# Keep phase-1 tensors and the FFN1 weights in one SBUF arena, and start three of the eight FFN1 weight groups inside phase 1

## The chip, the cores and the metric

The program runs on all 8 cores of one Trainium2 chip, with no exchange between them. Each core takes four prompt sequences of 256 tokens (1024 rows) and half of a sample's 1024 latent tokens (512 rows of its own, and the other 512 only as keys and values). All cores read the same weights from the chip's memory. The metric is device time in microseconds of the slowest core; lower is better.

## The reference, cut to what matters

One trunk layer: modulation vectors from `silu(cond) @ w_mod + b_mod` (six vectors: three for the attention half, three for the feed-forward half), then two residual sub-layers.

```
def _layer(x, mod, p, ctx_ckv=None, ctx_kr=None, rope=None):
    shift_a, scale_a, gate_a, shift_f, scale_f, gate_f = mod
    h = _rms(x, p['g_attn_pre']) * (1.0 + scale_a) + shift_a
    proj = h @ p['w_in']                      # -> q_lora | kv_lora | k_rope | sgu_u | sgu_v
    ...
    attn = _attend(q, k, val)                 # 8 heads, 64+32 dims
    sgu = _sgu(u, v, p['w_sgu'], p['b_sgu'], p['g_sgu'], p['beta_sgu'])
    mix = jnp.concatenate([attn, sgu], axis=-1) @ p['w_o']
    x = x + gate_a * _rms(mix, p['g_attn_post'])
    h = _rms(x, p['g_ffn_pre']) * (1.0 + scale_f) + shift_f
    f = jnp.square(jax.nn.relu(h @ p['w_ff1'])) @ p['w_ff2']
    x = x + gate_f * _rms(f, p['g_ffn_post'])
    return x, ckv, kr
```

`w_mod` is 1024 x 6144, `w_ff1` 1024 x 4096 and `w_ff2` 4096 x 1024, all f32 in memory. The kernel holds them as bf16.

## The kernel before, in words

The kernel is written as one program with a small recording helper (`KB`). Every operation names the tiles it reads and writes by strings; the helper puts a semaphore wait in front of it for the last writer (and readers) of each name. The order on each engine is the order of the Python code; nothing reorders it.

Three stages follow each other:

- **Stage A (L264 to L443)**: modulation for the attention half. Six slabs of `w_mod` (1024 x 512 each) come through two buffers `wm0`, `wm1`, beside `w_in`, `w_uq`, `w_ukv`, `w_sgu`, `w_o`, and the rotary tables `CT`, `ST` are computed in scratch tiles (`rowi`, `coli`, `ang`, `tmpa`, `m_`, `ti`).
- **Stage B (L445 to L760)**: the attention half. `front_A` loads and normalises 512 rows, `front_B` projects them (`w_in_bf`, `w_uq_bf`) and leaves keys, values and queries, `build_V` makes values, `attention` runs the heads, `sgu_and_out` the gating part and the output projection (`w_o_bf`). It runs once for the sample tokens and then for `g = 0` and `g = 1`, two groups of 512 prompt rows; in each of these, `attention` is called twice (`j = 0, 1`, 256 rows each). In that short-sequence form of `attention`, POOL first copies the rotary rows of all eight heads into the key tiles (`cp("pool", ...)`, L642), and DVE and ACT then cast the other 64 rows into the same tiles (L649, L651). Each cast writes the names `KT.h` that the copies wrote, so it waits for them.
- **Stage C (L762 to L815)**: a barrier of all engines, the close of the SBUF tiles of stages A and B, and the modulation for the feed-forward half: six more `w_mod` slabs, through the one buffer `wm2`. POOL issues all DMAs that convert f32 to bf16, in this order: slab 6, `w1.0`, `w2.0`, slab 7, `w1.1`, `w2.1`, ..., slab 11, `w1.5`, `w2.5`, `w1.6`, `w2.6`, `w1.7`, `w2.7`. Here `w1.g` is 512 columns of `w_ff1` and `w2.g` 512 rows of `w_ff2`, each 1 MiB as bf16, as is a slab. A slab's DMA waits until TensorE has read the slab before it, since the buffer is the same; TensorE's 16 matmuls of a slab (8 chunks for each of two conditions) wait until it has landed. SP issues the two broadcasts of `g_ffn_post` (`G_f`, 128 x 1024 f32 each) and one of `b_mod` a slab (`bm2`, 128 x 512 f32).
- **Stage D (L818 to the end)**: the feed-forward half, six groups of 256 rows. `ff1` and `ff2` are interleaved; chunk `fc` of 32 needs weight group `fc // 4` of both. The program ends with this stage's `tail`.

The loop that sets the order of stage C:

```
    mod2_dma(6)
    wgroup_dma(0)
    for j in range(6, 12):
        emit_mod2(j)
        if j + 1 < 12:
            mod2_dma(j + 1)
        wgroup_dma(j - 5)
    wgroup_dma(7)
    kb.barrier(exclude=("w1.", "w2."))
```

Of the kernel before, what the change touches and what calls it, by code (L numbers as in the profile page):

```python
# [14 lines left out]
D = 1024  # L15
# [124 lines left out]
def build_program(debug=False):  # L140
# [30 lines left out]
    w_ff1 = din("w_ff1", [D, 4 * D])  # L171
# [7 lines left out]
    kb = KB(nc)  # L179
# [26 lines left out]
    def mm(out, lhsT, rhs, start, stop):  # L206
        return lambda e: e.matmul(out, lhsT, rhs, start=start, stop=stop)  # L207
# [11 lines left out]
    def psf(i):  # L219
        return psb[i][:, :]  # L220
# [22 lines left out]
    kb.op("pool", lambda e: e.memset(eps_col[:], EPS), writes=["eps"])  # L243

    P1 = contextlib.ExitStack()
    w_in_bf = kb.sb(P1, "w_in_bf", [128, 8, 1440], BF16)
    wkr_pad = kb.sb(P1, "wkr_pad", [128, 8, 96], BF16)
    wkr_swp = kb.sb(P1, "wkr_swp", [128, 8, 96], BF16)
    w_uq_bf = kb.sb(P1, "w_uq_bf", [128, 2, 8, 96], BF16)
    w_uq_swp = kb.sb(P1, "w_uq_swp", [128, 2, 8, 96], BF16)  # L250
    w_ukv_bf = kb.sb(P1, "w_ukv_bf", [128, 8, 128], BF16)
    wsguT = kb.sb(P1, "wsguT", [128, 8, 128], BF16)
    w_o_bf = kb.sb(P1, "w_o_bf", [128, 8, D], BF16)
    G_a = kb.sb(P1, "G_a", [128, 2, D], F32)
# [3 lines left out]
    bT_bc = kb.sb(P1, "bT_bc", [128, 8, 128], F32)  # L258
    bTb = kb.sb(P1, "bTb", [128, 8, 128], BF16)
    cst_bf = kb.sb(P1, "cst_bf", [128, 128], BF16)  # L260
    CT = kb.sb(P1, "CT", [128, 1024], F32)
    ST = kb.sb(P1, "ST", [128, 1024], F32)

    kb.op("pool", lambda e: e.memset(cst_bf[:], 1.0 / 128.0), writes=["cst_bf"])  # L264

# [9 lines left out]
    kf = kb.sb(T0, "kf", [128, 1], F32)  # L275
    freq = kb.sb(T0, "freq", [128, 1], F32)
    isrow = kb.sb(T0, "isrow", [128, 1], F32)
    rowi = kb.sb(T0, "rowi", [128, 16, 64], F32)
    coli = kb.sb(T0, "coli", [128, 16, 64], F32)
    ang = kb.sb(T0, "ang", [128, 1024], F32)  # L280
    tmpa = kb.sb(T0, "tmpa", [128, 1024], F32)
    m_ = kb.sb(T0, "m_", [128, 1024], F32)
    ti = kb.sb(T0, "ti", [128, 1024], I32)
    wm = [kb.sb(T0, "wm%d" % i, [128, 8, 512], BF16) for i in range(2)]
    bm = [kb.sb(T0, "bm%d" % i, [128, 512], F32) for i in range(2)]
    mrow = [kb.sb(T0, "mrow%d" % i, [128, 512], F32) for i in range(2)]
# [157 lines left out]

    W1 = contextlib.ExitStack()  # L445
    hT = kb.sb(W1, "hT", [128, 8, 512], BF16)
    xq = kb.sb(W1, "xq", [128, 4096], BF16)
    uT = kb.sb(W1, "uT", [128, 4, 512], BF16)
    gv = kb.sb(W1, "gv", [128, 4, 512], F32)
    vn = kb.sb(W1, "vn", [128, 4, 512], BF16)  # L450
# [2 lines left out]
    ckvn_bf = kb.sb(W1, "ckvn_bf", [128, 4, 128], BF16)  # L453
    kr_f = kb.sb(W1, "kr_f", [128, 4, 32], F32)
    cqnT = kb.sb(W1, "cqnT", [128, 2, 512], BF16)
    ckvT = kb.sb(W1, "ckvT", [128, 1280], BF16)
    krT = kb.sb(W1, "krT", [128, 1280], BF16)
    KTh = [kb.sb(W1, "KTh%d" % i, [128, 1280], BF16) for i in range(2)]
    Vt = kb.sb(W1, "Vt", [128, 10, 512], BF16)
    PT = [kb.sb(W1, "PT%d" % i, [128, 512], BF16) for i in range(3)]  # L460
    rec = kb.sb(W1, "rec", [128, 512], F32)
    junk = kb.sb(W1, "junk", [128, 1024], BF16)
# [289 lines left out]
    for g in range(2):  # L752
        slots = [4 + 4 * g + t for t in range(4)]
        front_B(slots, 0, True, 0, None, g * 512)
        build_V([0, 1, 2, 3], lambda kt: kt * 128)
        for j in range(2):
            attention(j * 256, 256, j * 256, 256, 2 * j, j * 256)
        if g == 0:
            front_A(xp[512:1024, :], [8, 9, 10, 11])
        sgu_and_out(slots, 0, None)  # L760

    kb.barrier()  # L762
    W1.close()
    P1.close()

    P2 = contextlib.ExitStack()
    G_f = kb.sb(P2, "G_f", [128, 2, D], F32)
    w1_bf = kb.sb(P2, "w1_bf", [128, 8, 4 * D], BF16)
    w2_bf = kb.sb(P2, "w2_bf", [128, 32, D], BF16)
    for c in range(2):  # L770
        kb.dma("sp", G_f[:, c, :], g_ffn_post.partition_broadcast(128), "G_f%d" % c, True)
# [9 lines left out]
        kb.dma("sp", bm2[:], b_mod[j * 512:(j + 1) * 512].partition_broadcast(128), "bm2", True)  # L781

    def wgroup_dma(g):
        kb.dma("pool", w1_bf[:, :, g * 512:(g + 1) * 512], w_ff1[:, g * 512:(g + 1) * 512].rearrange("(kc p) n -> p kc n", p=128), "w1.%d" % g, True)
        kb.dma("pool", w2_bf[:, g * 4:(g + 1) * 4, :], w_ff2[g * 512:(g + 1) * 512, :].rearrange("(kc p) n -> p kc n", p=128), "w2.%d" % g, True)

    def emit_mod2(j):
# [64 lines left out]
    def ff1(sg, fc):  # L852
        hb_ = h2T[sg % 2]
        b = 2 + fc % 2
        r = fc % 2
        r4 = (sg * NFC + fc) % NH
        kb.group("pe", [mm(psf(b)[:, 0:256], w1_bf[:, kc, fc * 128:(fc + 1) * 128], hb_[:, kc, :], kc == 0, kc == 7) for kc in range(8)],
                 reads=["h2T%d.%d" % (sg % 2, kc) for kc in range(8)] + ["w1.%d" % (fc // 4)], writes=["ps%d" % b])
        act(rl[r][:, :], psf(b)[:, 0:256], AF.Relu, ["ps%d" % b], ["rl%d" % r])
        tt("dve", hid[r4][:, :], rl[r][:, :], rl[r][:, :], ALU.mult, ["rl%d" % r], ["hid%d" % r4])  # L860
# [119 lines left out]
```

How the kernel before makes its waits and increments, by code:

```python
    def _wait(self, engname, ev):  # L50
        if ev is None:
            return
        sem, val = ev
        w = self.waited[engname]
        if w.get(id(sem), 0) >= val:
            return
        w[id(sem)] = val
        self.eng[engname].wait_ge(sem, val)
        self.nwaits += 1
# [26 lines left out]
    def op(self, engname, fn, reads=(), writes=()):  # L86
        self._deps(engname, reads, writes)
        ins = fn(self.eng[engname])
        self.ecount[engname] += 1
        ev = (self.esem[engname], self.ecount[engname])
        ins.then_inc(ev[0], 1)
        self._record(ev, reads, writes)
        self.nops += 1
        return ev
# [1 line left out]
    def group(self, engname, fns, reads=(), writes=()):  # L96
        self._deps(engname, reads, writes)
        ins = None
        for fn in fns:
            ins = fn(self.eng[engname])
            self.nops += 1
        self.ecount[engname] += 1
        ev = (self.esem[engname], self.ecount[engname])
        ins.then_inc(ev[0], 1)
        self._record(ev, reads, writes)
        return ev
# [1 line left out]
    def dma(self, q, out, in_, res, write, **kw):  # L108
        reads = [] if write else [res]
        writes = [res] if write else []
        self._deps(q, reads, writes)
        if res not in self.dsem:
            self.dsem[res] = [self.stack.enter_context(self.nc.semaphore("d_" + res.replace(".", "_"))), 0]
        d = self.dsem[res]
        self.eng[q].dma_start(out=out, in_=in_, **kw).then_inc(d[0], 16)
        d[1] += 16
        ev = (d[0], d[1])
        self._record(ev, reads, writes)
```

## Time and profile before

| what | us |
|---|---|
| two runs of the kernel | 1116.92 and 1202.06, median 1159.49 |
| the profiled execution | 1120.75 |
| its span, slowest core (core 3) | 1119.7 |
| spans of the 8 cores | 1090.8 to 1119.7 |
| PE busy | 744.6 (67%) |
| DVE busy | 435.2 (39%) |
| ACT busy | 345.3 (31%) |
| POOL busy | 81.6 (7%) |

Times in the rows are counted from the span's start on the core that the row belongs to. "PE" is TensorE's matmul part. The page cuts the span in 40 slices of 28 us each; a digit is a busy share in tenths, so the row of DMA shows in which slices transfers run at all, and the row of GB/s what they moved. The chain of waits goes back from the last instruction to whatever released each step, and so names what the end of the program hangs on at each time.

### The profile page before, as it was taken

Reading aid. Unit: us, or ns where it says so; the run is one execution under the profiler, and the core shown is the slowest. Engines: PE = TensorE matmul, PEld = TensorE weight load, DVE = VectorE, ACT = ScalarE, POOL = GpSimd, SP = SyncE. Lnnn points to the kernel's source line nnn. Section 1 sums busy time; section 2 is a strip of 40 time slices with the busy share of each in tenths; the row PEclk is TensorE's granted clock in tenths of the full one; section 3 lists DMA queues with packets and bytes.
Section 4 is the critical chain, followed back from the end, with each engine's and each line's share of the span. In section 5 each row is a group of like instructions: output and inputs, shape, how many; then the busy total and the mean of one; then the engine's idle time right before and its main releaser. Section 6 shows DMA issues by size and latency. Waiting matters only on the chain.

```text
span 1119.7 us, 14484 instructions; the slowest of 8 cores (1090.8 to 1119.7 us)
## 1 busy us (share of the span) xinstructions
PE 744.6 (67%) x4097; PEld 409.8 (37%) x4097; DVE 435.2 (39%) x775; ACT 345.3 (31%) x815; POOL 81.6 (7%) x131
## 2 busy tenths in 40 slices
PE   2224158577767766667671242249999999999995
PEld 1001044122233333332340010027666665656663
DVE  2447231645654157531762123013242424242423
ACT  0000244444534454335421000024243433324322
POOL 3002000011101100010102001200000000000000
PEclk9566568779988865869576556559999999999998
DMA  8997700000000200000003999994000100000000
GB/s 140 167 141 110 230 14 1 0 1 1 1 1 1 88 1 1 1 13 1 1 1 60 162 156 144 151 164 84 2 39 1 39 1 39 2 38 2 31 8 39
DMA packets 38608, 58.05 MB, mean 52 GB/s; under 512 B 4322, under 2 KB 26244, under 8 KB 38532
## 3 DMA queue, kind: packets, MB, share of 16 engines
q0 software_dynamic: 29104, 35.41, 22.1%
q1 hardware_dynamic: 9428, 21.72, 6.9%
q8 instruction: 37, 0.61, 0.2%
q14 instruction: 39, 0.32, 0.1%
HBM read 85.58 MB, written 6.95 MB: 83 GB/s over the span
## 4 chain that ended last, share of the span: by engine, by line
PE 53%; DMA 17%; DVE 11%; ACT 9%; issue 7%; POOL 0%; ACTq 0%; DVEq 0%; SPq 0%; POOLq 0%
PE psb L207 51%; DMA wm<-w_mod 16%; ACT junk L190 3%; ACT PT L190 2%; DVE rec L626 2%; PE psb L210 2%; DVE hT L193 2%; DMA x<-xs 1%; ACT stat L190 1%; DVE xq L197 1%; DVE vn L193 1%; ACT L190 1%; DVE h2T L193 1%; DVE KTh L204 1%; ACT hT L190 1%
## 5 line engine op out<-in xcount | busy, mean ns | idle before, releaser
L207 PE MATMUL psb<-w_bf,hid 128*128 128x512 bf16 x768 | 198.8, 382 | 11.2 <-DVE xn L193 6.3
L207 PE MATMUL psb<-h2T,w_bf 128*128 128x256 bf16 x1536 | 201.8, 276 | 0.9 <-ACT h2T L190 0.9
L207 PE MATMUL psb<-wm,srep 128*128 128x512 bf16 x192 | 70.5, 549 | 171.1 <-DMA wm<-w_mod 164.6
L207 PEld LDWEIGHTS psb<-h2T,w_bf 128*128 128x128 bf16 x1536 | 151.8, 99 | 60.6 <-issue 2.2
L193 DVE TENSOR_TENSOR hid<-rl 128x256 bf16<-128x256 f32 x192 | 80.7, 425 | 222.1 <-PE psb L207 135.1
L190 ACT ACTIVATE rl<-psb 128x256 f32<-128x256 f32 x192 | 73.1, 384 | 223.0 <-PE psb L207 175.2
L207 PEld LDWEIGHTS psb<-wm,srep 128*128 128x128 bf16 x192 | 24.5, 132 | 216.6 <-issue 212.5
L207 PEld LDWEIGHTS psb<-w_bf,hid 128*128 128x128 bf16 x768 | 73.2, 98 | 64.1 <-issue 15.9
L190 ACT ACTIVATE PT<-psb 128x512 bf16<-128x512 f32 x112 | 65.4, 596 | 57.7 <-PE psb L207 54.7
L207 PE MATMUL psb<-PT,Vt 128*128 128x512 bf16 (+1 forms) x144 | 57.3, 398 | 28.2 <-ACT PT L190 13.7
L193 DVE TENSOR_TENSOR mrow<-psb,bm 128x512 f32<-128x512 f32 x24 | 16.6, 691 | 144.4 <-PE psb L207 143.4
L626 DVE RECIPROCAL rec<-psb 64x256 f32<-64x256 f32 (+1 forms) x24 | 54.8, 2284 | 18.8 <-PE psb L207 18.4
L190 ACT ACTIVATE junk<-psb 128x512 bf16<-128x512 f32 (+2 forms) x76 | 37.5, 494 | 69.6 <-PE psb L207 66.7
L207 PE MATMUL psb<-PT,ones_bf 128*128 128x512 bf16 (+1 forms) x144 | 58.3, 405 | 0.0
L190 ACT ACTIVATE xn<-x 128x1024 bf16<-128x1024 f32 x12 | 12.6, 1053 | 147.0 <-DVE G_f L193 146.4
L207 PE MATMUL psb<-w_in_bf,hT 128*128 128x416 bf16 (+2 forms) x224 | 49.5, 392 | 3.2 <-DVE hT L198 3.2
L207 PE MATMUL psb<-xq,KTh 96*128 96x512 bf16 (+1 forms) x144 | 50.0, 408 | 0.0
L207 PE MATMUL psb<-w_o_bf,hT 128*128 128x512 bf16 x192 | 43.7, 387 | 6.7 <-DVE hT L193 5.6
L190 ACT ACT_TABLE_LOAD x10 | 12.8, 1283 | 105.1 <-DVE tmpa L193 49.3
L207 PEld LDWEIGHTS psb<-PT,Vt 128*128 128x128 bf16 x144 | 16.4, 114 | 72.1 <-issue 68.0
L204 POOL COPY KTh<-krT 32x256 bf16<-32x256 bf16 (+1 forms) x40 | 21.8, 564 | 203.7 <-DVE KTh L204 115.0
L204 DVE CAST KTh<-psb 64x512 bf16<-64x512 f32 (+1 forms) x32 | 19.7, 616 | 39.6 <-PE psb L207 38.0
(158 smaller groups left out, 819.8 us busy)
## 6 DMA issues: line engine op xcount, KB each, us to landing
w_bf<-w_ff POOLq DMA_DIRECT2D x16, 1024.0 KB, 28.9
wm<-w_mod POOLq DMA_DIRECT2D x12, 1024.0 KB, 16.1
x<-xs SPq DMA_DIRECT2D x8, 512.0 KB, 13.1
x<-xp SPq DMA_DIRECT2D x8, 512.0 KB, 5.0
yp<-x SPq DMA_DIRECT2D x8, 512.0 KB, 2.6
bm<-b_mod SPq DMA_DIRECT2D x12, 256.0 KB, 9.0
w_in_bf<-w_in POOLq DMA_DIRECT2D x1, 2880.0 KB, 51.5
w_o_bf<-w_o POOLq DMA_DIRECT2D x1, 2048.0 KB, 26.2
```

The source lines that it names most:

```text
L190: return kb.op("act", lambda e: e.activation(out=out, in_=in_, func=func, **kw), reads, writes)
L193: return kb.op(eng, lambda e: e.tensor_tensor(out=out, in0=in0, in1=in1, op=op), reads, writes)
L197: return kb.op(eng, lambda e: e.tensor_scalar(out=out, in0=in0, scalar1=s1, scalar2=None, op0=op0), reads, writes)
L204: return kb.op(eng, lambda e: e.tensor_copy(out, in_), reads, writes)
L207: return lambda e: e.matmul(out, lhsT, rhs, start=start, stop=stop)
L210: return lambda e: e.transpose(out, in_, ident)
L626: kb.op("dve", lambda e: e.reciprocal(out=rec[po:po + 64, 0:nq], in_=den), reads=["ps%d" % pden], writes=["rec%d" % (h % 2)])
```

## The change

One tile `arena` (128 partitions x 32768 bf16, 64 KiB a partition) is allocated for the whole program in place of `w1_bf`. Its eight eighths hold `w1.0` to `w1.7` in stage C and D. In stages A and B its first part holds `w_in_bf`, `CT`, `ST`, `Vt`, `xq`, `KTh`, `ckvT`, `krT`, `w_uq_bf` and `w_ukv_bf`, in this order, and in stage A the scratch of the rotary tables lies over the part from `Vt` on. The first three groups of `w_ff1` lie over `w_in_bf` and the first part of `CT`.

The new function `w1_early` makes POOL wait for everything that the four compute engines have been given up to that place, and then issues the DMAs of `w1.0`, `w1.1` and `w1.2`. It is called in `g == 1`, behind the last `front_B` (the last reader of `w_in_bf`). Stage C issues only `w1.3` to `w1.7`, the barrier in front of it does not wait for the early ones, and `w1.g` now lies as [8][512] in its eighth instead of in columns of one wide tile.

```
@@ -223,6 +223,14 @@
     x1 = kb.sb(PS, "x1", [128, 12, D], F32)
+    arena = kb.sb(PS, "arena", [128, 32768], BF16)
+    _aoff = [0]
+
+    def aview(n_bf16):
+        o = _aoff[0]
+        _aoff[0] = o + n_bf16
+        assert _aoff[0] <= 32768
+        return arena[:, o:o + n_bf16]
@@ -243,12 +251,19 @@
-    w_in_bf = kb.sb(P1, "w_in_bf", [128, 8, 1440], BF16)
+    w_in_bf = aview(8 * 1440).rearrange("p (k n) -> p k n", k=8)
+    CT = aview(2048).bitcast(F32)
+    ST = aview(2048).bitcast(F32)
+    Vt = aview(10 * 512).rearrange("p (t n) -> p t n", t=10)
+    xq = aview(4096)
+    KTh = [aview(1280), aview(1280)]
+    ckvT = aview(1280)
+    krT = aview(1280)
+    w_uq_bf = aview(2 * 8 * 96).rearrange("p (c h d) -> p c h d", c=2, h=8)
+    w_ukv_bf = aview(8 * 128).rearrange("p (h d) -> p h d", h=8)
...
@@ -464,6 +473,15 @@
+    w1v = arena[:, :].rearrange("p (g k n) -> p g k n", g=8, k=8)
+
+    def w1_early(groups):
+        for e_ in ("pe", "act", "dve", "pool"):
+            if kb.ecount[e_] > 0:
+                kb._wait("pool", (kb.esem[e_], kb.ecount[e_]))
+        for g_ in groups:
+            kb.dma("pool", w1v[:, g_, :, :], w_ff1[:, g_ * 512:(g_ + 1) * 512].rearrange("(kc p) n -> p kc n", p=128), "w1.%d" % g_, True)
@@ -752,6 +770,8 @@
         front_B(slots, 0, True, 0, None, g * 512)
+        if g == 1:
+            w1_early([0, 1, 2])
         build_V([0, 1, 2, 3], lambda kt: kt * 128)
...
@@ -759,13 +779,12 @@
-    kb.barrier()
+    kb.barrier(exclude=("w1.",))
     W1.close()
     P1.close()
 
     P2 = contextlib.ExitStack()
     G_f = kb.sb(P2, "G_f", [128, 2, D], F32)
-    w1_bf = kb.sb(P2, "w1_bf", [128, 8, 4 * D], BF16)
     w2_bf = kb.sb(P2, "w2_bf", [128, 32, D], BF16)
@@ -781,7 +800,8 @@
     def wgroup_dma(g):
-        kb.dma("pool", w1_bf[:, :, g * 512:(g + 1) * 512], w_ff1[:, g * 512:(g + 1) * 512].rearrange("(kc p) n -> p kc n", p=128), "w1.%d" % g, True)
+        if g >= 3:
+            kb.dma("pool", w1v[:, g, :, :], w_ff1[:, g * 512:(g + 1) * 512].rearrange("(kc p) n -> p kc n", p=128), "w1.%d" % g, True)
         kb.dma("pool", w2_bf[:, g * 4:(g + 1) * 4, :], w_ff2[g * 512:(g + 1) * 512, :].rearrange("(kc p) n -> p kc n", p=128), "w2.%d" % g, True)
```

**POOL, stage B, `g == 1`, before and with the change.** The rows stand between the last cast of `ckvn_bf` in `front_B` and the residual add of `sgu_and_out`; `KTh<-krT` (now `arena<-arena`) are the copies of the rotary rows, eight for `j = 0` and eight for `j = 1`. Before:

```order
L204 CAST ckvn_bf<-ckvn_f 128x128 [waits s_dve,s_pool] x4
L204 COPY KTh<-krT 32x256 [waits s_dve,s_pe]
L204 COPY KTh<-krT 32x256 [waits s_pe]
L204 COPY KTh<-krT 32x256 [waits s_act,s_pe]
L204 COPY KTh<-krT 32x256 [waits s_pe] x3
L204 COPY KTh<-krT 32x256 [waits s_act,s_pe]
L204 COPY KTh<-krT 32x256 [waits s_pe]
```

With the change:

```order
L204 CAST ckvn_bf<-ckvn_f 128x128 [waits s_dve,s_pool] x4
L115 DMA arena<-w_ff 128x8x512 [waits s_pe,s_act,s_dve,s_pool]
L115 DMA arena<-w_ff 128x8x512 x2
L204 COPY arena<-arena 32x256 x8
L204 COPY arena<-arena 32x256 [waits s_dve,s_pe]
L204 COPY arena<-arena 32x256 [waits s_pe]
```

Three DMA issues and their wait for all four engines now stand ahead of the eight copies of `j = 0`.

**POOL, stage C.** The difference in the order, from the residual adds at the end of stage B on; `wm` is the slab, `w_bf 128x8x512` (now `arena`) a group of `w_ff1` and `w_bf 128x4x1024` one of `w_ff2`:

```order
 L193 TENSOR_TENSOR x<-x,gv 128x512 x4
 L115 DMA wm<-w_mod 128x8x512
-L115 DMA w_bf<-w_ff 128x8x512
 L115 DMA w_bf<-w_ff 128x4x1024
 L115 DMA wm<-w_mod 128x8x512
-L115 DMA w_bf<-w_ff 128x8x512
 L115 DMA w_bf<-w_ff 128x4x1024
 L115 DMA wm<-w_mod 128x8x512
-L115 DMA w_bf<-w_ff 128x8x512
 L115 DMA w_bf<-w_ff 128x4x1024
```

Behind slabs 6, 7 and 8 stands one weight group instead of two. From slab 9 on the order is the same as before.

## Rows read from the trace of the kernel before

**Rows 1.** The page, 40 slices of the span: granted TensorE clock, DMA share, GB/s.

```profile
PEclk9566568779988865869576556559999999999998
DMA  8997700000000200000003999994000100000000
GB/s 140 167 141 110 230 14 1 0 1 1 1 1 1 88 1 1 1 13 1 1 1 60 162 156 144 151 164 84 2 39 1 39 1 39 2 38 2 31 8 39
```

**Rows 2.** The view of all cores: span and mean granted clock.

```profile
core 0: 1090.8 us, clock 0.813
...
core 3: 1119.7 us, clock 0.802
```

**Rows 3.** Chain of waits, core 3: start, us, engine and tile; a DMA's length is issue to landing.

```profile
601.37 20.18 DMA wm<-w_mod
621.69 5.83 PE psb L207 x16
628.04 16.20 DMA wm<-w_mod
...
651.62 14.28 DMA wm<-w_mod
...
672.51 16.08 DMA wm<-w_mod
...
695.96 15.99 DMA wm<-w_mod
...
719.56 14.06 DMA wm<-w_mod
733.96 6.01 PE psb L207 x16
...
752.15 22.86 PE psb L207 x156
```

**Rows 4.** Stretches, core 3: busy by engine, then granted clock, DMA share, GB/s.

```profile
600.00:622.00 22.00, 0.31 (x1) 0.14 (x2) 0.00 (x0) 0.00 (x0) 2.56 (x3) 0.50 0.80 121
622.00:740.00 118.00, 36.40 (x96) 12.45 (x94) 25.60 (x62) 0.00 (x0) 15.88 (x19) 0.59 1.06 153
...
753.00:760.00 7.00, 7.00 (x49) 5.20 (x48) 2.13 (x5) 2.31 (x6) 0.00 (x0) 0.79 1.17 208
...
800.00:1119.00 319.00, 297.00 (x2046) 197.84 (x2044) 108.58 (x226) 106.40 (x280) 0.00 (x0) 0.98 0.05 21
```

**Rows 5.** DMA issues of 602.2:603.0 and of 628.9:629.7 (w1.0, w1.1), us to landing.

```profile
w_bf<-w_ff POOLq DMA_DIRECT2D x1, 1024.0 KB, 28.2
...
w_bf<-w_ff POOLq DMA_DIRECT2D x1, 1024.0 KB, 23.8
```

**Rows 6.** One stretch of core 0, columns as in Rows 4.

```profile
590.00:600.00 10.00, 2.37 (x6) 0.90 (x7) 0.00 (x0) 0.00 (x0) 0.00 (x0) 0.50 1.21 214
```

**Rows 7.** Chain of waits, core 0.

```profile
585.59 11.91 DMA wm<-w_mod
...
723.87 6.68 PE psb L207 x48
```

**Rows 8.** Timeline of POOL, core 3: start, us for all of the row's instructions.

```profile
503.01 2.79 POOL L204 COPY KTh<-krT 32x256 bf16<-32x256 bf16 x8 [7.02 <-DVE krT L204]
...
602.29 1.64 POOL L115 DMA_DIRECT2D w_bf<-w_ff  x2
...
720.43 4.92 POOL L115 DMA_DIRECT2D w_bf<-w_ff  x6
```

**Rows 9.** Timeline of core 3 where attention of `g = 1`, `j = 0` begins.

```profile
529.32 0.20 ACT L190 ACTIVATE stat<-stat 128x4 f32<-128x4 f32 x1
...
531.13 0.68 DVE L204 CAST KTh<-psb 64x512 bf16<-64x512 f32 x1 [1.63 <-PE psb L207]
...
532.26 0.59 ACT L190 ACTIVATE KTh<-psb 64x512 bf16<-64x512 f32 x1 [0.93 <-PE psb L207]
...
534.28 1.06 ACT L190 ACTIVATE PT<-psb 128x512 bf16<-128x512 f32 x2
```

More of the change, by code:

```diff
@@ L245, in build_program @@
     P1 = contextlib.ExitStack()
-    w_in_bf = kb.sb(P1, "w_in_bf", [128, 8, 1440], BF16)
+    w_in_bf = aview(8 * 1440).rearrange("p (k n) -> p k n", k=8)
[8 more added lines that the diff above has]
+    w_ukv_bf = aview(8 * 128).rearrange("p (h d) -> p h d", h=8)
     wkr_pad = kb.sb(P1, "wkr_pad", [128, 8, 96], BF16)
     wkr_swp = kb.sb(P1, "wkr_swp", [128, 8, 96], BF16)
-    w_uq_bf = kb.sb(P1, "w_uq_bf", [128, 2, 8, 96], BF16)
     w_uq_swp = kb.sb(P1, "w_uq_swp", [128, 2, 8, 96], BF16)
-    w_ukv_bf = kb.sb(P1, "w_ukv_bf", [128, 8, 128], BF16)
     wsguT = kb.sb(P1, "wsguT", [128, 8, 128], BF16)
@@ L260, in build_program @@
     cst_bf = kb.sb(P1, "cst_bf", [128, 128], BF16)
-    CT = kb.sb(P1, "CT", [128, 1024], F32)
-    ST = kb.sb(P1, "ST", [128, 1024], F32)
     kb.op("pool", lambda e: e.memset(cst_bf[:], 1.0 / 128.0), writes=["cst_bf"])
@@ L277, in build_program @@
     isrow = kb.sb(T0, "isrow", [128, 1], F32)
[L278 to L283, printed above, removed]
+    _sb = 15616
+    rowi = arena[:, _sb:_sb + 2048].bitcast(F32).rearrange("p (a b) -> p a b", a=16)
+    coli = arena[:, _sb + 2048:_sb + 4096].bitcast(F32).rearrange("p (a b) -> p a b", a=16)
+    ang = arena[:, _sb + 4096:_sb + 6144].bitcast(F32)
+    tmpa = arena[:, _sb + 6144:_sb + 8192].bitcast(F32)
+    m_ = arena[:, _sb + 8192:_sb + 10240].bitcast(F32)
+    ti = arena[:, _sb + 10240:_sb + 12288].bitcast(I32)
     wm = [kb.sb(T0, "wm%d" % i, [128, 8, 512], BF16) for i in range(2)]
@@ L446, in build_program @@
     hT = kb.sb(W1, "hT", [128, 8, 512], BF16)
-    xq = kb.sb(W1, "xq", [128, 4096], BF16)
     uT = kb.sb(W1, "uT", [128, 4, 512], BF16)
@@ L455, in build_program @@
     cqnT = kb.sb(W1, "cqnT", [128, 2, 512], BF16)
[L456 to L459, printed above, removed]
     PT = [kb.sb(W1, "PT%d" % i, [128, 512], BF16) for i in range(3)]
@@ L856, in ff1 @@
         r4 = (sg * NFC + fc) % NH
-        kb.group("pe", [mm(psf(b)[:, 0:256], w1_bf[:, kc, fc * 128:(fc + 1) * 128], hb_[:, kc, :], kc == 0, kc == 7) for kc in range(8)],
+        kb.group("pe", [mm(psf(b)[:, 0:256], w1v[:, fc // 4, kc, (fc % 4) * 128:(fc % 4 + 1) * 128], hb_[:, kc, :], kc == 0, kc == 7) for kc in range(8)],
                  reads=["h2T%d.%d" % (sg % 2, kc) for kc in range(8)] + ["w1.%d" % (fc // 4)], writes=["ps%d" % b])
```

## The prediction, made before the changed kernel was run

> **What bounds the kernel now.** I read the page's slices first. DMA is busy in three places only: the first 140 us, a single slice near 370 us, and slices 22 to 28, about 600 to 770 us [rows 1]. In the last of these the granted TensorE clock stands at its lower level of 1.2 GHz (digits of 5 and 6), because TensorE mostly waits. Next come the cores: the slowest is core 3 with 1119.7 us, the fastest core 0 with 1090.8 [rows 2]. The sum is made against core 3.
>
> Then the chain of waits in order of time. From 601.37 us it is six times the same link: a `w_mod` slab is issued, lands 20.18, 16.20, 14.28, 16.08, 15.99 and 14.06 us later, and TensorE works some 6 us on it before the next slab can be issued into the same buffer [rows 3]. The reader should see that TensorE's 16 matmuls are the small part, and that a slab of 1 MiB takes twice as long as it should. At the 153 GB/s of that stretch [rows 4] a slab (1.049 MB) and its `bm2` (0.262 MB) need 8.6 us. The rest is what stands in front: `w1.1` was issued at 628.9 us and landed 23.8 us later [rows 5], at 652.7, after slab 8 had been issued at 651.62, and `w2.1` stood behind it. So POOL's queue is served in order, and 5.5 to 7.6 us of weights lie ahead of each slab. DMA share is 1.06 in this stretch: transfers bound stage C. Behind it, stage D runs from 752.15 us [rows 3] to the end at the upper clock level with PE busy for 297 of 319 us [rows 4]; it is TensorE's own and of fixed length.
>
> **What is taken out of stage C.** Three DMAs of 1.049 MB leave the queue, behind slabs 6, 7 and 8. By bytes alone that is 3.15 MB / 153 GB/s = 20.6 us. Step by step, on core 3:
> - Slab 6 lands as before, near 621.6: ahead of or beside it are only `G_f` (2 x 0.524 MB), `bm2` and itself, 2.36 MB, which at 121 GB/s [rows 4] take 19.5 us of the 20.18. Slab 7 goes out at 628.04. Until then 22 x 0.121 + 6 x 0.153 = 3.6 MB have moved, against 4.46 MB issued before and 3.41 MB now, so it finds an empty queue: 8.6 + 0.7 (20.18 less 19.5, the start) = 9.3 us in place of 16.20.
> - From a landing to the next issue it is 6.5 to 7.6 us [rows 3], 7.1 as a mean. So slabs 8 and 9 are issued at 644.4 and 660.8 (before 651.62 and 672.51). Each period now holds 2.36 MB, 15.4 us at 153 GB/s, within its 16.4 us, so both land in 9.3 us.
> - Behind slab 9 two groups follow again. Slab 10 is issued at 677.2 (before 695.96) with 3.41 - 16.4 x 0.153 = 0.90 MB ahead and needs 14.5 us; slab 11 is issued at 698.8 (before 719.56) with 1.0 MB ahead, needs 15.2, and lands at 714.0 instead of 733.6.
>
> **Gain 19.6 us**, just under the 20.6 by bytes, since the queue is nearly full even in the short periods. First the row: core 3 shares the chip with seven others, and its rate in this stage is 153 GB/s written, twice that read since the source is f32 [rows 4]. The Trainium skill (HBM Reference, Specifications) gives each of two paired cores about 358 GB/s; as an estimate from that page this would be 179 GB/s written, and the removed bytes would be worth 17.6 us and not 20.6. The measured rate decides here.
>
> **What is late next.** Stage D starts about 18 us sooner, near 734 us. The last three pairs of groups (6.3 MB, 41 us) follow slab 11, so the last lands near 755 us. Stage D takes 1119.7 - 752.15 = 367.6 us for 192 chunks, 1.91 us each, so group 5 is asked for 38 us and group 7 54 us after its start, 772 and 788. No new wait. In 753 to 760 us PE was busy for 7.00 of 7.00 us beside 208 GB/s [rows 4], so transfers beside it cost it nothing.
>
> **What is put into stage B.** POOL's wait is over when ACT ends the last `stat` of `front_B`, 529.32 + 0.20 = 529.5 us [rows 9]. A pair of issues takes 1.64 us and six take 4.92 [rows 8], so three end at 532.0. Only then come the eight key copies, 2.79 us together [rows 8], which before had been done at 503 us, long ahead of need. The first two end at 532.8, the fourth at 533.5, the eighth at 534.9. The casts that wait for them began at 531.13 (DVE) and 532.26 (ACT) [rows 9]; now at 532.85 and 533.55. The second of them holds the PSUM bank that the fourth key product needs, and the fourth cast waits for the eighth copy, so the first exponentials slip from 534.28 [rows 9] to about 535.6. **Cost 1.5 us**, bounds 0 and 5 (nearly the whole of issues plus copies, 2.5 + 2.8). It is on the path: from here to the barrier one engine waits for the other. SP issues nothing here.
>
> A row first: beside DVE's casts nothing of POOL's issuing shows in stage B; the issues that are seen take 0.82 us each [rows 8]. The Trainium skill (SBUF — State Buffer, SBUF: two separate sides) holds that POOL cannot write its descriptors while DVE runs an operation in a two-port mode. By that rule each issue might wait out one 0.69 us cast, an estimate of 2 us more, and the sum would be 1105. No row here shows it.
>
> The early transfers themselves take 14.7 us (at core 0's 214 GB/s [rows 6]) to 20.6 us, from 530 to at most 553. The DMA row is empty there until 600 us [rows 1], which is the cover: 47 us. The 1 KiB runs per weight row stay what they were; the other tiles moved into the arena keep their names and so their waits; the rotary scratch in the arena is used as before. They add no instruction, and I cost them at nothing.
>
> **Sum.** 1120.75 - 19.6 + 1.5 = 1102.65, so **1103 us** for an execution like the profiled one (1.6% less). The median shown, 1159.49, lies 3.5% above the profiled execution because one of its two runs took 1202.06; the other took 1116.92. My numbers are for executions like 1116.92 and 1120.75. A measurement of this kernel tells about 2%, 22 us, from no change.
>
> **Rivals.**
> 1. *The transfers get faster too.* Core 0 came first to stage C, at 585.59 us, had 214 GB/s [rows 6] and its first slab in 11.91 us [rows 7], where core 3 needed 20.18. If every core had 190 GB/s all along, slab 6 would land after 12 us, slabs 7 to 9 after 7.6, slabs 10 and 11 after some 10.5, and with 7.1 us between each landing and the next issue slab 11 would land 12 + 3 x 7.6 + 2 x 10.5 + 5 x 7.1 = 91 us after the first issue instead of 132: 1081. 25 MB less over eight cores may bring them half way there, **1092**. Against: the short periods still ask 144 GB/s on each core, so the load hardly falls. 0.17.
> 2. *The slab hardly waits for those bytes.* If slab and later groups are served side by side, or latency and not queue makes the 16 us, each of three periods loses only what lies between the slab's landing and the next issue. For it: `w1.0` landed 28.2 us after issue [rows 5], 9 us behind slab 6, more than its own 6.9. I put the gain at 3 us a period, 9 in all, net 7: **1113**. 0.10.
> 3. *Slower: the clock in stage D.* Stage D runs at 0.98 granted clock [rows 4], after 150 us in which TensorE mostly rested. If a shorter rest made the chip grant less, its 367.6 us would stretch. Below 0.934 the gain is gone (367.6 x 0.98 / 0.934 = 385.7); at 0.90 it is +33, net +15, **1135**; past 0.88 it is more than 2% slower. Against: core 0 spent 138 us from its first slab to stage D (585.59 to 723.87 [rows 7]) and core 3 151 us, and stage D took 366.9 and 367.6 us. 0.04.
> 4. *The early weights aren't early*, because POOL reaches its wait late or the new barrier holds it up: no gain, plus 1.5: **1122**. Against: the order of POOL's rows; POOL is idle there. 0.03.
>
> **Chances and range.** The forecast has 0.66, with a range of its own of 1096 to 1109: gain 13 to 24 in stage C (20.6 us at 153 GB/s; 26 at 121; less if periods grow), cost 0 to 5. The whole range is 1090 to 1118: it takes in the second rival and the near half of the first. Faster by over 2% (below 1098) are the first rival and the best part of the forecast, 0.16 + 0.08 = 0.24; slower by over 2% is the far part of the third, 0.02; the rest, 0.74, is within 2%.
>
> **What would show it.** Between landing of slab 7, 8 and 9 and their issues 9 to 10 us instead of 14 to 16; slabs 10 and 11 nearly as before. DMA busy in slice 19 or 20. The stretch from first slab issue to stage D 131 us instead of 151. On POOL three issues of about 0.8 us near 531 us and then eight copies; the first exponentials 1 to 2 us later against the end of `front_B`. Stage D 367 us. I am wrong if the slabs still take 14 us or more with an empty queue, if the rate rises above 180 GB/s, or if stage D changes length.

## The result: 0.8% faster, in the range but less than forecast

The changed kernel takes 1108.09 us (median of 15 executions), the kernel before 1118.31 us (median of 14). The ratio is **0.9917, 95% interval 0.9893 to 0.9941**. The 1159.49 us shown ahead came from one of its two executions, at 1202.06; such executions, which both kernels have, are left out of every ratio here. The forecast was 1103 us with 1090 to 1118, and "within 2%" as the likeliest outcome.

The page of the changed kernel, with the three rows that answer to [rows 1], shows that the early transfers are where they were put: the 20th slice has become busy, and slices 22 to 26, the first of stage C, move fewer bytes than before (54 to 147 GB/s; [rows 1] have 60 to 162). The transfers still end in the 28th slice on this core.

```profile
PEclk9666578779988865869567566569999999999998
DMA  8997700000000200000802889994000000000000
GB/s 147 163 143 124 229 1 1 0 1 1 1 1 3 86 1 1 1 13 1 114 1 54 106 132 134 147 158 82 1 39 1 39 1 39 2 38 2 36 4 39
```

The view of all cores answers to [rows 2]. The cores have changed places: the slowest is now core 1, and core 3 (1089.8 us) is among the fast ones. Which core is slow is a matter of the execution, so a comparison of one core with itself misleads here.

```profile
core 1: 1114.0 us, clock 0.807
...
core 4: 1088.5 us, clock 0.814
```

I therefore cut each core's span at four places that its trace shows (the last cast of `ckvn_bf` in `front_B`, the issue of slab 6, the first FFN1 matmul, the end) and took the mean over the eight cores. "B end" goes from that cast to the issue of slab 6; it holds all that the early issues could disturb.

```
mean of 8 cores, us    B end   stage C   stage D   mean span
before                 105.8   145.9     367.3     1108.9
changed                109.9   131.6     367.3     1100.0
```

So stage C gives 14.3 us, stage B takes 4.1, stage D is untouched, and 10.2 us should be left. The medians differ by 10.2 us, the ratio stands for 9.3, and the two mean spans differ by 8.9, because the part ahead of the first cut came out 1.4 us longer. Each row is one execution of each kernel, and stage C differs by some 3 us between executions of the same queue order (145.9, 143.1 and 142.7 further down), so the 14.3 us is good to about that, and the exact match with the medians is luck. Forecast for the three were 19.6, 1.5 and 0.

**Stage C.** The chain of waits of core 1, columns as in [rows 3]. Its stage C, 144.0 us, is the longest of the eight; the shortest is 123.3.

```profile
602.94 18.54 DMA wm<-w_mod
621.62 6.24 PE psb L207 x16
628.38 15.10 DMA wm<-w_mod
...
649.76 12.55 DMA wm<-w_mod
...
669.38 12.35 DMA wm<-w_mod
...
687.83 18.30 DMA wm<-w_mod
...
713.60 15.58 DMA wm<-w_mod
```

And two of core 3's rows in the same execution:

```profile
617.72 10.55 DMA wm<-w_mod
...
635.08 10.69 DMA wm<-w_mod
```

The reader should see the second to fourth slab: 15.10, 12.55 and 12.35 us on one core and 10 to 11 on the other, where [rows 3] have 14 to 16. As a mean of the cores, issue to landing went as follows.

```
slab            6      7      8      9      10     11
before          16.0   16.4   15.4   15.4   14.8   15.8
changed         15.4   12.0   10.8   11.2   15.3   16.1
forecast        20.2    9.3    9.3    9.3   14.5   15.2   (for core 3)
```

The stretch 622 to 740 us of core 1, as in [rows 4], now has less than a full DMA share, 0.92 and 132 GB/s against 1.06 and 153. The queue runs dry between slabs, so this is a mean over full and empty times; a rate while the queue is full stands further down:

```profile
622.00:740.00 118.00, 34.03 (x96) 11.81 (x94) 27.14 (x65) 2.79 (x6) 14.10 (x17) 0.63 0.92 132
```

**Stage B.** POOL's timeline of core 1, which answers to [rows 8], has three issues and then the eight copies, which before were done at 505.80 us, 25 us ahead of the first cast that needs them ([rows 8], [rows 9]):

```profile
527.54 2.68 POOL L115 DMA_DIRECT2D arena<-w_ff  x3 [34.20 <-ACT arena L190]
530.26 2.79 POOL L204 COPY arena<-arena 32x256 bf16<-32x256 bf16 x8
```

The rows that answer to [rows 9] show the hand-over: both casts now wait for POOL.

```profile
531.10 0.68 DVE L204 CAST arena<-psb 64x512 bf16<-64x512 f32 x1 [4.24 <-POOL arena L204]
...
531.77 0.59 ACT L190 ACTIVATE arena<-psb 64x512 bf16<-64x512 f32 x1 [3.10 <-POOL arena L204]
...
533.80 1.06 ACT L190 ACTIVATE PT<-psb 128x512 bf16<-128x512 f32 x2
```

From the last table load of `front_B` (524.99 us here, 527.63 before) to these exponentials it is 8.8 us; before it was 6.65 (to 534.28 in [rows 9]). That is 2.2 us. Most of the other 2 stands some 45 us later in the output projection. The chain of core 3 before and of core 1 now, one row each:

```profile
579.23 7.08 PE psb L207 x32
```

```profile
579.12 8.76 PE psb L207 x32
```

Same 32 matmuls, 1.7 us longer. The windows view of these microseconds and of the four ahead of them says why (granted clock in the third column from the end; 1.00 is the upper level, 2.4 GHz, 0.50 the lower, 1.2 GHz). Before:

```profile
575.00:579.00 4.00, 1.81 (x29) 1.49 (x27) 3.62 (x6) 0.00 (x0) 0.00 (x0) 1.00 0.00 0
579.00:583.00 4.00, 3.77 (x18) 1.79 (x19) 0.08 (x1) 0.80 (x3) 0.00 (x0) 1.00 0.01 4
```

Now:

```profile
575.00:579.00 4.00, 1.78 (x25) 1.53 (x22) 3.34 (x5) 0.00 (x0) 0.00 (x0) 0.91 0.00 0
579.00:583.00 4.00, 3.88 (x11) 1.48 (x12) 0.00 (x0) 0.21 (x1) 0.00 (x0) 0.57 0.02 4
```

In both kernels the clock is at the lower level while TensorE works on the gating part, and reaches the upper one 3 to 4 us ahead of the projection. Then TensorE rests for about 2 us. Before, the clock stays up through the projection. Now it falls again as the projection begins and is back some 3.5 us later. It is a second fall, not a first rise that comes late. Where the expectations below say that the clock "comes back later in the output projection", this fall is what they mean.

### The profile page after: what moved, and what is told of

It reads as the page before. It is cut to its first block, busy times and chain, and to the rows that moved or that the text cites. A ratio compares the mean times of both kernels' runs of the same rounds, so it can differ in the third digit from the quotient of the medians.

```text
span 1114.0 us, 14477 instructions; the slowest of 8 cores (1088.5 to 1114.0 us)
## 1 busy us (share of the span) xinstructions
PE 743.6 (67%) x4097; PEld 409.7 (37%) x4097; DVE 435.1 (39%) x775; ACT 345.1 (31%) x815; POOL 81.6 (7%) x131
## 4 chain that ended last, share of the span: by engine, by line
PE 54%; DMA 16%; DVE 12%; ACT 9%; issue 7%; POOL 1%; DVEq 0%; ACTq 0%; POOLq 0%
PE psb L207 52%; DMA wm<-w_mod 14%; ACT junk L190 3%; ACT PT L190 2%; DVE rec L644 2%; PE psb L210 2%; DVE arena L204 1%; DVE hT L193 1%; DMA ck_ld<-ckr 1%; DVE arena L197 1%; ACT stat L190 1%; DVE vn L193 1%; DVE h2T L193 1%; ACT arena L190 1%; ACT L190 1%
## 5 line engine op out<-in xcount | busy, mean ns | idle before, releaser
L207 PE MATMUL psb<-w_bf,hid 128*128 128x512 bf16 x768 | 198.8, 382 | 11.2 <-DVE xn L193 6.3
L207 PE MATMUL psb<-h2T,arena 128*128 128x256 bf16 x1536 | 201.4, 275 | 0.9 <-ACT h2T L190 0.9
L207 PE MATMUL psb<-wm,srep 128*128 128x512 bf16 x192 | 66.4, 522 | 166.6 <-DMA wm<-w_mod 148.8
L207 PEld LDWEIGHTS psb<-h2T,arena 128*128 128x128 bf16 x1536 | 151.6, 99 | 60.4 <-issue 2.2
L207 PE MATMUL psb<-arena 96*128 96x512 bf16 (+3 forms) x218 | 72.9, 412 | 32.3 <-DVE arena L204 25.1
L207 PE MATMUL psb<-PT,arena 128*128 128x512 bf16 (+1 forms) x144 | 57.3, 398 | 28.3 <-ACT PT L190 14.1
L204 DVE CAST arena<-psb 64x512 bf16<-64x512 f32 (+4 forms) x51 | 32.8, 644 | 100.9 <-PE psb L207 57.0
L207 PE MATMUL psb<-arena,hT 128*128 128x416 bf16 (+2 forms) x224 | 49.1, 389 | 3.2 <-DVE hT L198 3.2
L207 PEld LDWEIGHTS psb<-arena 96*128 96x128 bf16 (+1 forms) x218 | 24.4, 117 | 63.5 <-issue 49.1
L207 PEld LDWEIGHTS psb<-PT,arena 128*128 128x128 bf16 x144 | 16.4, 114 | 72.2 <-issue 68.1
## 6 DMA issues: line engine op xcount, KB each, us to landing
wm<-w_mod POOLq DMA_DIRECT2D x12, 1024.0 KB, 15.4
x<-xs SPq DMA_DIRECT2D x8, 512.0 KB, 11.5
```

The lines of the kernel that those rows point to most:

```text
L204: return kb.op(eng, lambda e: e.tensor_copy(out, in_), reads, writes)
```

## The experiments

The theory after the result: stage C gave less than forecast because a slab's own landing costs more than I put down, and stage B cost more because POOL's copies stand behind the issues, which also makes the clock fall in the output projection. Each was set against rivals. One table holds the stage means of one execution each and the ratios; the run with long rows is read by its landings alone. Neither that run nor the one with one bias row computes the layer: each leaves a part out.

```
kernel                          B end  stage C  stage D   ratio to before (95%)
changed                         109.9  131.6    367.3     0.9917 (0.9893 to 0.9941)
nothing early                   106.0  143.1    367.7     0.9997 (0.9973 to 1.0020)
issued behind the copies        105.8  129.2    367.4     0.9849 (0.9822 to 0.9876)
slabs 6 to 9 alone in queue     109.9  127.2    367.4     0.9867 (0.9838 to 0.9897)
four groups early               109.3  124.5    367.3     0.9837 (0.9802 to 0.9873)
slabs first                     109.9   67.9    388.7     0.9532 (0.9503 to 0.9560)
slabs first, nothing early      105.7   67.6    409.0     0.9694 (0.9662 to 0.9726)
all together                    105.7   67.9    379.7     0.9427 (0.9398 to 0.9455)
delay only, nothing early       109.6  142.7    367.4     1.0062 (1.0035 to 1.0088)
slabs alone, one bias row       109.9  116.8    367.8     0.9802 (0.9763 to 0.9841)
```

### Nothing early

```
-            w1_early([0, 1, 2])
+            w1_early([])
...
-        if g >= 3:
+        if g >= 0:
```

> The arena, its addresses and POOL's wait behind the last front_B are kept, but no weight group is issued early; stage C issues all eight groups of w_ff1 as before the change. Theory (only the moved transfers matter): the stretch from the last ckvn_bf cast to the first slab issue is 105.7 us on nearly every core, as before, stage C is about 146 us as a mean of the cores, and the time is within 0.5% of the kernel before. Rival (the tiles' new places in SBUF cost something): the stretch stays near the 109.9 us of the changed kernel, and the time is 0.3% or more above the kernel before.

Measured: B end 106.0, stage C 143.1 (145.9 before; such means differ by some 3 us between executions), ratio 0.9997. The arena, its addresses and POOL's wait cost nothing that can be measured; all of the effect, both signs, comes from the three moved issues and their transfers. The rival falls.

### Issued behind the key copies

The call moves into `attention`, behind the loop of the eight copies.

```
-        if g == 1:
-            w1_early([0, 1, 2])
...
                 cp("pool", kbuf[64:96, kc0:kc0 + nk], krT[64:96, k0:k0 + nk], krblk, ["KT.%d" % h_])
+            if behind_copies is not None:
+                behind_copies()
...
-            attention(j * 256, 256, j * 256, 256, 2 * j, j * 256)
+            attention(j * 256, 256, j * 256, 256, 2 * j, j * 256, (lambda: w1_early([0, 1, 2])) if (g, j) == (1, 0) else None)
```

> The three early issues stand behind the eight key copies of j = 0 instead of ahead of them. Theory (the copies queued behind POOL's issues cost stage B its 4.2 us, 2.2 directly at the start of attention and 2 because the TensorE clock comes back later in the output projection): the stretch from the last ckvn_bf cast to the first slab issue falls from 109.9 to 105.7 to 107 us on all cores, stage C stays near 132 us as a mean, and the time is 3 to 4 us below the changed kernel, 0.988 of the kernel before. Rival (the 2 us in the output projection come from the transfers running beside attention): it falls only to about 107.9. Second rival (all 4.2 us come from the transfers): it stays at 109.9.

Measured: B end 105.5 to 105.7 on seven of eight cores (107.0 on one), ratio 0.9849 against 0.9917, where 0.988 was expected. POOL's timeline of core 3 shows the issues in their new place, and its chain the output projection at its old length:

```profile
526.51 2.68 POOL L115 DMA_DIRECT2D arena<-w_ff  x3 [26.18 <-DVE arena L204]
529.16 0.77 POOL L204 COPY arena<-arena 32x256 bf16<-32x256 bf16 x2
```

```profile
573.76 7.08 PE psb L207 x32
```

The transfers still run beside attention and cost it nothing. Stage C, 129.2 us, has the queue order of the changed kernel, whose 131.6 it differs from by no more than executions do. The core with 107.0 us has the long output projection (8.56 us), with nothing queued ahead of its copies. All 4.1 us were the price of queueing compute behind three DMA issues, and none of it had to be paid. Both rivals fall.

### Delay only

Three clears of dead tiles take the place of the three issues; POOL waits for them, then come the copies.

```
-            w1_early([0, 1, 2])
+            w1_early([])
+            for nm_, t_ in (("w_uq_swp", w_uq_swp), ("wkr_pad", wkr_pad), ("wkr_swp", wkr_swp)):
+                kb.op("pool", lambda e, t_=t_: e.memset(t_[:], 0.0), writes=[nm_])
+            kb._wait("pool", (kb.esem["pool"], kb.ecount["pool"]))
```

> No weight group is issued early, but POOL clears three tiles that nobody reads any more at the same place, ahead of the key copies of j = 0, about 2.7 us as long as the three issues. Theory (the clock in the output projection comes back later because the start of attention is delayed, not because transfers run beside it): the stretch from the last ckvn_bf cast to the first slab issue is 109 to 110 us, as with the change, and stage C about 145 us. Rival (delay and transfers are both needed): 107.5 to 108.

Measured: B end 109.6 on all cores but one (109.7), without a single transfer. From the table load to the first exponentials it is 8.5 us, 1.9 more than before. The ratio, 1.0062 (1.0035 to 1.0088), has the 3.8 us at the lower end of its interval. The chain of core 3 has the long output projection again:

```profile
573.07 8.77 PE psb L207 x32
```

The clock falls there as in the changed kernel:

```profile
573.00:577.00 4.00, 3.93 (x11) 1.48 (x12) 0.00 (x0) 0.58 (x1) 0.00 (x0) 0.57 0.02 4
```

So some 2 us of delay at the start of attention suffices to make the clock fall again in the output projection, 45 us behind it, and that costs some 2 us more. The traces of all runs show how far this reaches. The long projection (8.4 to 8.8 us, against 6.9 to 7.1) stands on all 48 cores of the six runs with three issues or three clears ahead of the copies, and on 4 of 40 where the copies come first or nothing is issued early: one core of the kernel before (its 107.0 us), two with nothing early, one with the issues behind the copies. So the fall occurs without the delay too, but rarely; with it, it is the rule. Why, no run here tells. (The run with four issues stands apart; see there.)

### Slabs alone in the queue

```
     def wgroup_dma(g, late=False):
...
+        if g < 3 and not late:
+            return
         kb.dma("pool", w2_bf[:, g * 4:(g + 1) * 4, :], ...
...
+        if j == 11:
+            for g_ in range(3):
+                wgroup_dma(g_, True)
         wgroup_dma(j - 5)
```

> w2.0, w2.1 and w2.2 are issued behind slab 11 and w1.5, w2.5, so that slabs 6 to 9 have POOL's queue to themselves. Theory (a slab's own bytes are slow, about 115 GB/s with its bias rows, whatever follows it in the queue): slabs 7, 8 and 9 still take 9.5 to 11 us from issue to landing against 10 to 12.5. Rival (the group issued 0.9 us behind a slab is served beside it): they fall to 7.5 us or less. Slab 6 should then fall by more than the others, since G_f goes beside it. The sum of bytes is the same, and stage D may now wait for w2.0, so that the time is about that of the changed kernel, 0.985 to 1.0 of the kernel before.

Measured, issue to landing for slabs 6 to 9 as means of the cores: 12.1, 9.8, 10.2, 11.7 us, against 15.4, 12.0, 10.8, 11.2. One core's chain:

```profile
611.83 9.88 DMA wm<-w_mod
...
629.07 10.37 DMA wm<-w_mod
```

An empty queue ahead and behind still leaves 9.8 to 10.2 us: the group issued behind a slab is not served beside it, or only little. What it takes is 2.2 us of slab 7, 0.6 of slab 8 and 3.3 of slab 6 against the changed kernel, and 1.4, 0.3 and 1.6 against the run with the issues behind the copies, which has the same order in stage C (13.7, 11.2 and 10.5 us); up to half of these amounts is then a matter of the execution. Slab 9 has lost `w2.2` ahead of it here and keeps two groups behind it, as with the change, and is no better off: 11.7 us is above what was expected (9.5 to 11), 9.9 to 10.5 us on four cores and 12.7 to 14.5 on the other four. Stage D, 367.4 us, waited for none of the late groups.

### One bias row

```
-        kb.dma("sp", bm2[:], b_mod[j * 512:(j + 1) * 512].partition_broadcast(128), "bm2", True)
+        if j == 6:
+            kb.dma("sp", bm2[:], b_mod[j * 512:(j + 1) * 512].partition_broadcast(128), "bm2", True)
```

> As the run with slabs 6 to 9 alone in POOL's queue, but only slab 6 loads bias rows; slabs 7 to 11 add slab 6's bias (their part of the computation is left out). It tells what the 0.26 MB broadcast beside each slab costs. Theory (it costs its bytes, 1.7 us at 153 GB/s, or about 2 at the slab's own rate): slabs 7, 8 and 9 land in 8 to 8.5 us instead of 9.5 to 10.5, stage C is 4 to 6 us shorter, about 122 us as a mean. Rival (a slab alone is what takes 9.5 to 10 us; the broadcast goes beside it for nothing): 9.5 us or more. Second rival (the broadcast holds the slab up out of proportion): 7 us or less.

Measured, in two executions: slabs 7 and 8 in 8.2 and 8.3 us. The broadcast costs each of them 1.6 to 1.9 us, its bytes and no more. A slab by itself takes 8.2 us. Stage C is 116.8 us, 10.4 less than with all bias rows, where 4 to 6 were expected: slabs 9, 10 and 11, with groups in the queue, gained 2.2, 1.6 and 2.7 us (slab 9 took 9.5 us, not 8 to 8.5). Why they gained more than the bytes of a broadcast is open.

```profile
610.57 8.28 DMA wm<-w_mod
...
625.25 8.29 DMA wm<-w_mod
```

### Long rows

Each slab's DMA reads 512 whole rows of `w_ff2` instead of pieces of `w_mod`.

```
-        kb.dma("pool", wm2[:], w_mod[:, j * 512:(j + 1) * 512].rearrange("(kc p) n -> p kc n", p=128), "wm2", True)
+        kb.dma("pool", wm2[:, :, :].rearrange("p k n -> p (k n)").rearrange("p (k n) -> p k n", k=4), w_ff2[(j - 6) * 512:(j - 5) * 512, :].rearrange("(kc p) n -> p kc n", p=128), "wm2", True)
```

> As the run with slabs 6 to 9 alone in POOL's queue, but each slab's DMA reads 512 whole rows of w_ff2, 4 KiB each, in place of 1024 pieces of 2 KiB out of w_mod (the second modulation is so left out). Theory (a slab is slow because of its short pieces; w2 groups landed some 5 us apart in a full queue where w1 groups took 8 to 9): slabs 7, 8 and 9 land in 7 to 8 us instead of 9.5 to 10.5. Rival (a megabyte alone takes that long whatever its rows, by start, rate limit and neighbours): 9.5 us or more.

Measured: slabs 7 and 8 in 9.4 and 9.5 us as means, 0.4 to 0.7 less than with short pieces, from one execution. My theory (7 to 8) falls; the rival (9.5 or more) holds but for 0.1 us.

```profile
631.52 9.63 DMA wm<-w_ff
```

### Four groups early

`w_uq_bf` goes beside `CT` and `ST`, the rotary scratch moves up by its size, and:

```
-            w1_early([0, 1, 2])
+            w1_early([0, 1, 2, 3])
...
-        if g >= 3:
+        if g >= 4:
```

> w_uq_bf is placed beside CT and ST in the arena, so that four eighths are dead behind the last front_B, and w1.0 to w1.3 are all issued there. Theory (each group of w_ff1 taken out of stage C saves some 5 us there, and each issue ahead of the key copies costs 0.9 us at the start of attention): stage C falls by 4 to 6 us to about 127 us as a mean, stage B's last stretch grows from 109.9 to 110.8, net 0.3 to 0.5% below the changed kernel, 0.987 of the kernel before. Rival (stage C is no longer bound by what stands in the queue but by each slab's own landing and TensorE's work): stage C falls by less than 2 us and the time doesn't fall.

Measured: stage C 124.5, 7.1 us less than with three groups; slab 10 now lands in 11.5 us instead of 15.3. Against the 129.2 us of the run with three groups behind the copies it is 4.7 us less, so a group taken out of a slab's way is worth about 5 to 7 us, and executions don't tell that from the 4.8 us a group that the first three gave.

B end was expected at 110.8 us and is 109.3 as a mean. The direct delay grew as expected: from the table load to the first exponentials it is 9.7 us, 3.0 more than before. But the clock falls in the output projection on three cores only; the other five keep it up. A core with the short projection and one with the long one:

```profile
576.40 7.08 PE psb L207 x32
```

```profile
577.17 8.66 PE psb L207 x32
```

The five have 108.7 or 108.8 us, the three 110.1 to 110.3. Four issues ahead of the copies thus cost five of eight cores less than three did: a longer delay isn't always a dearer one.

### Slabs first

If slabs are what the chain waits for, the better change is to the order of the queue. All six slabs are issued at once, into places that no weights fill yet; the weight groups follow. The second text below is for the same order with nothing issued before stage C.

```
+    def slab(j):
+        if j == 6:
+            return wm2[:, :, :], "wm2"
+        if j < 11:
+            return w1v[:, j - 3, :, :], "w1.%d" % (j - 3)
+        return w2_bf[:, 28:32, :].rearrange("p a n -> p (a n)").rearrange("p (k n) -> p k n", k=8), "w2.7"
...
+    kb.dma("sp", bm_all, b_mod[6 * 512:12 * 512].partition_broadcast(128), "bm_all", True)
...
+    for j in range(6, 12):
+        mod2_dma(j)
+    for g in range(4):
+        wgroup_dma(g)
+    for j in range(6, 12):
+        emit_mod2(j)
+    for g in range(4, 8):
+        wgroup_dma(g)
```

> As the changed kernel, but all six slabs are issued at once at the start of stage C, into tiles that no weight fills yet (the old slab buffer, the last four eighths of the arena and the place of w2.7), the six bias rows come as one broadcast, and all other weight groups are issued behind them. Theory (stage C's length is the bytes that stand ahead of slab 11 plus six times a round trip of landing, TensorE and issue): 8.9 MB instead of 16.7 MB go ahead of slab 11 and the round trips overlap, so slab 11 lands some 60 to 70 us after the first issue and stage C takes 80 to 88 us; the 13.6 MB behind it end 150 to 160 us after the first issue, group 7 is asked for at 138, and stage D grows from 367 to 375 to 390 us. Stage B stays at 109.9 us. Time 0.97 of the kernel before (0.96 to 0.98). Rival (transfers bound C and D together, so that what C gives D takes): C + D stay near 495 us, the time is 0.99.

> Slabs first, but no weight group is issued before stage C. It tells what the early groups are worth once no slab waits for a weight group: 16.8 MB follow the slabs instead of 13.6, so they end 175 to 185 us after the first issue. Theory (then the early groups are worth their bytes in stage D, 3.15 MB or some 20 us): stage B 105.7 us, stage C 80 to 88, stage D 395 to 410, the time 0.98 to 0.985 of the kernel before. Rival (stage D keeps up with the weights as they land, so that early groups are worth nothing): stage D within 5 us of that of the run with three early groups, time 0.965.

Measured: stage C falls by half, to 67.9 us; stage D grows by 21.4 to 388.7; ratio 0.9532, below the 0.96 to 0.98 expected. The chain of core 3 has one long wait for the last slab in place of six:

```profile
602.41 0.92 POOL wm L115
603.33 3.46 POOL arena L115 x4
606.79 49.45 DMA w_bf<-w_mod
656.59 3.63 PE psb L207 x16
...
672.51 23.55 PE psb L207 x156
```

Slab 11 lands at 656.24, 53.8 us after the first issue: 8.9 MB at 165 GB/s. I had expected 60 to 70 us, at 130 to 150 GB/s. With nothing early, stage C is the same (67.6) and stage D takes 409.0, 20.3 us more for 3.15 MB: the early groups are then worth their bytes at 155 GB/s. Its ratio, 0.9694, is also below what was expected (0.98 to 0.985). The rival of that run (nothing) falls; so does the one of the first (C + D is 456.6, not 495).

This edit changes two things: what stands ahead of the slabs, and that six slabs no longer take turns in one buffer, each waiting for TensorE to read the one before. No run has the order alone. An estimate from the rows: with slab 6 at 12.1 us, five more at the 10 us of an empty queue, and the 50.8 us of stage C in the changed kernel that are not landings, the stage would take 113 us. By that some 19 of the 64 us belong to the order and some 45 to the slabs landing one behind the other without a round trip.

### All together

Slabs first, four early groups, issued behind the key copies.

> Slabs first as in the run beside it, four early groups instead of three, and the early issues behind the key copies of j = 0. If the three gains add (4.2 us in stage B, 1 MB less behind the slabs, the slabs' 25 us): stage B's last stretch 105.7 us, stage C 80 to 88 us, stage D 370 to 382 us, the time 0.958 of the kernel before (0.95 to 0.97). Rival (stage D's granted clock falls because TensorE waits for weights in its first 60 us): stage D over 390 us and no gain over the run beside it.

Measured: B end 105.7, stage C 67.9, stage D 379.7, **1049.68 us, ratio 0.9427 (0.9398 to 0.9455)**, 5.7% below the kernel before. On the page DMA is dense from the 24th to the 28th slice, and the clock's digits reach 8 and 9 within them:

```profile
PEclk9767567959998785586956858799999999999998
DMA  8999810000000020000083199998101001010101
```

The gains add, and to more than I had put down (0.958, with 0.95 to 0.97). Stage D's clock suffers little: 0.94 in the 92 us in which weights still arrive, with PE busy for 81.6 us of them, where the first 92 us of stage D had 0.98 and 89.6 on core 3 before; 0.97 behind it:

```profile
668.00:760.00 92.00, 81.61 (x540) 54.65 (x549) 27.35 (x58) 29.39 (x76) 0.00 (x0) 0.94 0.74 116
760.00:1046.00 286.00, 264.00 (x1803) 177.46 (x1834) 94.51 (x198) 93.93 (x247) 0.00 (x0) 0.97 0.05 20
```

## Why the prediction was right in kind and off in size

**What bounds the kernel: right.** Stage C hangs on slabs that stand behind weights in one queue. Slabs 7 to 9 fell from 15 to 16 us to 11 to 12, and slabs 10 and 11 stayed, as the step had it. Rival 3 (the clock in stage D) is refuted by 367.3 us on both sides and rival 4 (not early) by the 20th slice of the page. Rival 1 (faster transfers) did not come: in full it wanted slab 6 in 12 us and slabs 7 to 9 in 7.6, and they took 15.4 and 11 to 12. Rival 2 (the slab hardly waits for those bytes) put the gain at 3 us a period; slabs 7, 8 and 9 gained 4.4, 4.6 and 4.2. Its total of 9 us is as far from the measured 14.3 as the forecast's 19.6 is. What refutes it as a mechanism is the run with the slabs alone: a group behind slabs 7 and 8 takes 2.2 us of them at most, so most of the old wait was for what stood ahead.

**The gain in stage C: the term that was mis-sized, 19.6 forecast, 14.3 measured.** First, a slab in an empty queue was put at 9.3 us, from the bytes at 153 GB/s. Alone it takes 9.8 to 10.2 (8.2 for itself and 1.6 to 1.9 for its bias rows), and with a group behind it and neighbours at work 10.8 to 12.0: over three slabs 34.0 us instead of 27.9, 6.1 us short. The empty queue's own rate is some 2 of these, the other traffic some 4. Second, slab 10 was to gain 1.5 us and lost 0.5. Against these 8 us stand some 3 that went better: slab 6 fell by 0.6, slab 11 lost 0.3 and not 1.1, and 1.3 us lie outside the landings. That I reckoned on core 3 doesn't explain the miss: its slabs 7 to 9 took 46.6 us before, those of the mean core 47.2. Its stage C was longer (150.8 against 145.9) through slab 6, 20.18 us against 16.0, which the forecast left as it was. So the 131 us on record for stage C, which meets the measured mean of 131.6, is luck.

The Trainium skill's pair share (HBM Reference, Specifications), by which the bytes were worth 17.6 us, goes by a rate of 179 GB/s written. The changed kernel's stage C shows rates on both sides of it while the queue is full. Core 1 has 160 GB/s at 680 to 690 us. Ten microseconds each on core 3, which came to stage C early, and on core 4:

```profile
600.00:610.00 10.00, 0.00 (x0) 0.00 (x0) 0.00 (x0) 0.00 (x0) 0.67 (x1) 0.50 1.07 221
```

```profile
640.00:650.00 10.00, 3.58 (x10) 1.35 (x11) 0.04 (x1) 0.00 (x0) 0.00 (x0) 0.53 1.13 199
```

Over all cores, the stretches of 5 us from 15 us after slab 6's issue on in which the DMA share was 1.05 or more have 171 GB/s as a mean, 166 before. That the skill's 17.6 us came nearer than 20.6 is no support for it: the gain fell short through single landings, not through the rate of a full queue.

**The cost in stage B: 1.5 forecast, 4.1 measured.** The mechanism was right and its place: casts wait for copies behind three issues. One row was misread on the way: the old copies were done at 505.80 us, not at 503, where they began; nothing hangs on it. The direct part was 2.2 us, since POOL started 0.7 us after ACT's last `stat` and each hand-over added a tenth or two. The other 2 us were not in the sum: the clock's second fall, in the output projection. I had written that the cost stays within 0 and 5, and it did. The Trainium skill's rule (SBUF — State Buffer, SBUF: two separate sides), by which DVE's work could hold up descriptor writing, was not put to the test here: on core 1 DVE was idle from 526.86 to 531.10 us, all through the three issues. With the issues behind the copies one cast fell among them:

```profile
527.30 0.68 DVE L204 CAST arena<-psb 64x512 bf16<-64x512 f32 x1 [0.98 <-PE psb L207]
```

They took 2.68 us there too, 0.89 each, against 0.82 in [rows 8]. The estimate of 2 us more doesn't show.

**Late next: right.** Stage D takes 367.3 us as before; no weight was late.

**Sum.** -14.3 + 4.1 = -10.2 us. On record: -18. The measured 1108 lies within the forecast's own 1096 to 1109, near its end: both terms missed to the same side, by 5.3 and 2.6 us.

## What to carry to other kernels

Ask first which transfer the path waits for and what stands ahead of it in its queue. Taking three of sixteen weight groups out of the way was worth 14 us; issuing all awaited slabs ahead of the weights, each into its own place, was worth 64 in that stage and 42 net, with the same bytes. And look at what is queued behind an early prefetch on the engine that issues it: the same three DMAs, behind the copies instead of ahead of them, gave 0.9849 instead of 0.9917.

## What was not expected of the hardware

- A delay of some 2 us at one place made a phase 45 us later run 1.7 us longer, on all eight cores alike, because the granted clock fell from 1.00 to 0.50 a second time as that phase began. With transfers and without delay it happened on one core of eight; with delay and without transfers on all eight; with a delay of 3.0 us on three.
- A 1 MiB bf16 slab (2 MiB read as f32) landed 8.2 us after its issue in an empty queue with all eight cores at work. With a bias broadcast beside it it took 9.8 to 10.2 us where the pieces read were 2 KiB, and 9.4 to 9.5 where they were 4 KiB.
- The core that is slowest changes from one execution to the next by what it meets in the DMA phases: stage C of one kernel went from 123.3 to 144.0 us over its eight cores. Where the metric is the slowest core, the mean over cores tells of an edit what one core's trace does not.
